# Meta rows side by side, a router fed by unnormed tokens, and the token-row step moved into the experts

## The reference, cut to what matters

```
h = modulate(rms_norm(x, g_ffn[l]), sh_f, sc_f)       # rms * g * (1 + sc) + sh
x = x + gt_f[:, None, :] * moe(h, w_router[l], b_router[l], w1, b1, w2, b2)
return rms_norm(x, g_final)

def moe(h, w_router, b_router, w1, b1, w2, b2):
    logits = xf @ w_router + b_router                 # 256 x 32
    top_val, top_idx = lax.top_k(logits, TOP_K)       # 4 of 32
    gates = jax.nn.softmax(top_val, axis=-1)
    # for each expert e, on its tokens:
    u = xb @ w1[e] + b1[e]
    glu = jnp.minimum(u[:, ::2], 7.0); lin = jnp.clip(u[:, 1::2], -7.0, 7.0)
    a = glu * jax.nn.sigmoid(1.702 * glu) * (lin + 1.0)
    y = a @ w2[e] + b2[e]                             # times its gate, added into x
```

## Time and profile before

| | us |
|---|---|
| median of 3 runs | 1924.18 |
| lowest and highest | 1923.88, 1926.73 |
| the profiled execution: its time | 1924.68 |
| its span, first to last instruction | 1923.0 |
| PE busy | 1826.4 (95%) |
| DVE busy, ACT busy | 800.5 (42%), 593.7 (31%) |
| transfers | 568.65 MB, mean 296 GB/s |

### The profile page before, as it was taken

How to read it: one execution, slowest core, us unless ns; L and a number is a source line. 1 busy time by engine, 2 the same in 40 slices (tenths; PEclk the granted TensorE clock), 3 DMA queues, 4 the chain that set the end, 5 groups by cost and what they waited for, 6 DMA issues and landing times.

```text
span 1923.0 us, 27611 instructions
## 1 busy us (share of the span) xinstructions
PE 1826.4 (95%) x11191; PEld 1224.0 (64%) x11192; DVE 800.5 (42%) x1357; ACT 593.7 (31%) x949; POOL 38.0 (2%) x62
## 2 busy tenths in 40 slices
PE   7999999989998999999899999999999999999996
PEld 6777779989998899899854344344344343343442
DVE  5444556778874544547412122222122122122222
ACT  5665676453435456555410000000000000000001
POOL 2000000000000000000000000000000000000000
PEclk9999999989998999999889999999999999999998
DMA  8333335768783744435759999999999999999995
GB/s 253 98 107 109 111 110 175 241 213 278 273 304 111 250 161 154 153 126 169 292 211 417 428 429 428 429 428 429 428 428 429 428 429 429 428 428 428 429 427 229
DMA packets 147813, 568.65 MB, mean 296 GB/s; under 512 B 6016, under 2 KB 102376, under 8 KB 123040
## 3 DMA queue, kind: packets, MB, share of 16 engines
q1 hardware_dynamic: 139616, 536.60, 70.8%
q0 software_dynamic: 8128, 31.07, 4.7%
HBM read 566.58 MB, written 3.43 MB: 296 GB/s over the span
## 4 chain that ended last, share of the span: by engine, by line
PE 58%; DMA 33%; ACT 4%; DVE 3%; issue 1%; SPq 0%; DVEq 0%; ACTq 0%
DMA s_ring<-in_w_mlp 33%; PE banks L2078 10%; PE banks L1692 9%; PE banks L1694 8%; PE banks L1693 8%; PE banks L1837 3%; PE banks L1838 3%; PE banks L1839 3%; PE banks L2115 3%; PE banks L2088 2%; PE banks L1650 1%; PE banks L2063 1%; ACT r_w2h L718 1%; DVE r_w2l L1110 0%; PE banks L1736 0%
## 5 line engine op out<-in xcount | busy, mean ns | idle before, releaser
L2078 PE MATMUL banks<-s_ring,s_W 128*64 128x512 f32 x2048 | 460.9, 598 | 29.5 <-DMA s_ring<-in_w_mlp 29.5
L2078 PEld LDWEIGHTS banks<-s_ring,s_W 128*64 128x64 f32 x2048 | 139.1, 137 | 331.6 <-issue 258.6
L1046 ACT ACTIVATE s_W<-s_W 128x512 f32<-128x512 f32 x32 | 20.2, 630 | 764.2 <-DVE s_W L1564 764.2
L2115 PE MATMUL banks<-s_ring,s_W 128*64 128x512 f32 x1024 | 226.0, 594 | 0.3 <-ACT s_W L1039 0.3
L1556 DVE TENSOR_TENSOR s_W<-banks,s_W 128x512 f32<-128x512 f32 x32 | 22.1, 692 | 461.0 <-PE banks L2115 461.0
L2115 PEld LDWEIGHTS banks<-s_ring,s_W 128*64 128x64 f32 x1024 | 73.3, 137 | 147.2 <-issue 132.7
L1338 DVE TENSOR_TENSOR r_w2l<-s_ring,r_w2h 128x1024 fp32r<-128x1024 f32 x96 | 116.9, 1223 | 83.3 <-ACT r_w2h L894 83.1
L1110 DVE TENSOR_TENSOR r_w2l<-s_ring,r_w2h 128x1024 fp32r<-128x1024 f32 x88 | 107.5, 1224 | 99.7 <-ACT r_w2h L718 99.2
L1543 DVE TENSOR_TENSOR s_W<-banks,s_W 128x512 f32<-128x512 f32 x128 | 82.2, 684 | 147.7 <-PE banks L2063 147.7
L1692 PE MATMUL banks<-r_x2h,r_w2h 128*128 128x256 f32 x448 | 130.8, 292 | 6.2 <-DVE r_x2l L1354 6.2
L2088 PEld LDWEIGHTS banks<-s_W 128*128 128x128 f32 x1024 | 120.0, 196 | 24.2 <-issue 24.2
(11 more groups left out here) (417 smaller groups left out, 3236.7 us busy)
## 6 DMA issues: line engine op xcount, KB each, us to landing
s_ring<-in_w_mlp SPq DMA_DIRECT2D x192, 2048.0 KB, 22.4
s_ring<-in_w_in SPq DMA_DIRECT2D x62, 1024.0 KB, 5.2
s_ring<-in_w_ada POOLq DMA_DIRECT2D x24, 1024.0 KB, 9.2
s_ring<-in_w_ffn_gate SPq DMA_DIRECT2D x11, 1024.0 KB, 5.4
s_ring<-in_w_ffn_up SPq DMA_DIRECT2D x11, 1024.0 KB, 10.6
s_ring<-in_w_ffn_down SPq DMA_DIRECT2D x5, 2048.0 KB, 10.1
s_ring<-in_w_gate SPq DMA_DIRECT2D x8, 1024.0 KB, 5.3
s_ring<-in_w_br_sb SPq DMA_DIRECT2D x4, 1024.0 KB, 4.8
```

Of the source, the lines that this page charges most:

```text
L2078: last = mm(pb[b][64 * h:64 * h + 64, :], XgT[:, 2 * c + k, :], slot(c, 2)[:, k, 1024 * h + 512 * b:1024 * h + 512 * b + 512], start=False ...
L2115: last = mm(pb[2][64 * h:64 * h + 64, :], aT[:, k, 64 * c:64 * c + 64], slot(4 + c, 4)[:, k, 512 * h:512 * h + 512], start=c == 0 and k == ...
```

## The change

In the first block: the rounded meta rows and their rest are laid side by side (`xm`, 32 columns), so that the meta part of an `sv` or `dv` unit has four products, not six; the meta keys are copied eight times over 128 columns (`skM`, on ACT), as is the triangle (`ntriM`), so that the meta rows of the stick-breaking steps fill 128 partitions and ACT and DVE take 640 columns in one instruction; of the differential steps the meta columns are doubled (`wvM`, on DVE), so that 32 rows sum both halves.

In the second block: the router weights and their bias are scaled by the norm's gain and shift while `o` runs (`router` and `router_bias`, at "wrA" and "wrB"); PE makes the logits from the unnormed residual, one slice behind the squares (`token_square`, `logits`), and the root is taken for each token (two columns). The token rows for the experts are a matmul of `hx` by a diagonal of the gains, scaled by the root when ACT copies them; the shift is added later, on DVE, when `XgT` is copied (`shifted`). Masks and gates are made with broadcast operations over all four choices. The spreads of the output gate come after the counts. The residual rows and the second biases move behind `expert(0)` (`first_sum`), the biases with four row groups of 32. `choose_g(e)` moves into turn e. The final gain is spread by PE at the very end and read by DVE from the banks.

```diff
@@ order2
-                 (unit_of("o") + 2, 1, SQUARED, {"square": 0}))
+                 (unit_of("o") + 2, 1, SQUARED, {"square": 0}),
+                 (unit_of("o"), 1, 1, {"wrA": 1.5, "wrB": 2.5}))
@@ ACT, first block
+        act.activation(xm[:, :, 0:M], xnm, ACT.Copy).then_inc(S["xn_hi"], 1)
...
+                act.activation(skM[:, c, :].rearrange("p (a n) -> p a n", a=KT), copies(src[:, 0:M]), ACT.Copy)
...
-                st.do(act.activation(ex[:, 0:384], ex[:, 0:384], ACT.Exp))
-                st.do(act.activation(ex[0:M, 384:640], ex[0:M, 384:640], ACT.Exp))
+                st.do(act.activation(ex, ex, ACT.Exp))
...
@@ ACT, before the experts
-        root(4, nrms, T)
-        for t in range(KT):
-            act.wait_ge(S["norm_x"], 3 * KT + t + 2)
-            act.activation(hn[:, t, :], hn[:, t, :], ACT.Identity, bias=modT[:, 24 + t:25 + t]).then_inc(S["norm_s"], 1)
-
-        act.wait_ge(S["b1_in"], 64)
+        act.wait_ge(S["norm_ms"], 6)
+        act.activation(root4, pb[3][:, 0:2], ACT.Sqrt, bias=epsc, scale=1.0 / D).then_inc(S["norm_r"], 1)
+        act.wait_ge(S["b1_in"], 128)
         act.activation(b1r[:, :], b1x, ACT.Copy).then_inc(S["b1_split"], 1)
...
         def expert(e, cur, prev):
-            if cur:
-                act.wait_ge(S["gath"], e + 1)
-                since(act, "u_mm", e * 4)
-                act.activation(XgT, pb[3].rearrange("p (a n) -> p a n", a=KT), ACT.Copy).then_inc(S["xg"], 1)
@@ DVE, before the experts
+        choose_b(0)
+        gates()
+        nc.vector.memset(taken, 0.0).then_inc(S["round"], 1)
...
+        tt(b2q, b2q, gty, ALU.mult).then_inc(S["b2_scaled"], 1)
         expert(0, True, False)
@@ DVE, a turn
         def expert(e, cur, prev):
-            if prev:
-                since(dve, "selt_mm", e - 1)
-                choose_g(e - 1)
             if cur:
                 dve.wait_ge(S["gath"], e + 1)
+                since(dve, "u_mm", e * 4)
+                shifted().then_inc(S["xg"], 1)
                 choose_u(e + 1)
+                since(dve, "selt_mm", e)
+                choose_g(e)
@@ PE, first block
             if kind in V_KINDS:
+                for kk in range(2):
+                    for i, w in enumerate((whi, wlo)):
+                        last = mm(pb[groups[0] % 3][0:2 * M, :], xm[:, 2 * (n % 4) + kk, :], w[:, kk, :],
+                                  start=n % 4 == 0 and kk + i == 0, stop=n % 4 == 3 and kk + i == 2)
...
@@ PE, second block
+        def logits(k):
...
+            last = mm(pb[5][0:E, 0:T], wrg[:, k, :], hx[:, k, :], start=k == 0, stop=k == KT - 1)
...
+        def token_square(k):
+            if k >= 1:
+                logits(k - 1)
+            if k == KT - 1:
+                logits(k)
+            pe.wait_ge(S["norm_sq"], KT * 3 + k + 1)
+            for t in range(2):
+                last = mm(pb[3][:, t:t + 1], nsq[:, k, P * t:P * t + P], ones[:, 0:1], start=k == 0 and t == 0, stop=k == KT - 1, skip_group_check=True)
...
+        def first_sum():
+            pe.wait_ge(S["route"], 6)
+            for t in range(2):
+                last = nc.tensor.transpose(pb[2][:, P * t:P * t + P], gat4[:, t, :], ident)
+            last.then_inc(S["gt_mm"], 1)
+            for b in range(4):
+                for j in range(4):
+                    mm(pb[4 + b][:, P * j:P * j + P], hx[:, 4 * (b % 2) + j, P * (b // 2):P * (b // 2) + P], ident,
+                       start=j == 0, stop=False, skip_group_check=True)
+            pe.wait_ge(S["gt_kept"], 1)
+            pe.wait_ge(S["b2_scaled"], 1)
+            for q in range(4):
+                v, t = slice(E * q, E * q + E), q % 2
+                mm(pb[4 + 2 * t + q // 2], gatT[v, P * t:P * t + P], b2q[v, :], start=False, stop=True, skip_group_check=True)\
+                    .then_inc(S["h_mm"], 1)
...
+        pe.wait_ge(S["spread_kept"], 2)
         expert(0, True, False)
-
-        pe.wait_ge(S["acc_init"], 4)
-        for b in range(2):
-            spread(6 + b, vec[:, VROW["g_final"]:VROW["g_final"] + KT], b).then_inc(S["spread"], 1)
+        first_sum()
         expert(1, True, True)
...
         further(pe, again)
+        for b in range(2):
+            spread(4 + b, vec[:, VROW["g_final"]:VROW["g_final"] + KT], b)
```

More of the change, by code:

```diff
@@ L306, in program @@
     mT = area(W, 20864, KT, T)
+    skM, ntriM, wvM = area(W, 20864, HEADS, P), W[0:M, 21888:22016], area(W, 22016, 2, 2 * M)
     zs, ex, sp, la = (lent[:, 640 * n:640 * n + 640] for n in range(4))
@@ L759, in keep1, with copies @@
             act.activation(dst, src, ACT.Copy, scale=scale).then_inc(S["act_evac1"], 1)
+        def copies(ap):
+            return ap.unsqueeze(1).broadcast_to([ap.shape[0], KT, M])
         def sb_step(s, h):
@@ L1048, in _ @@
         expert(0, True, False)
-        for b in range(2):
-            act.wait_ge(S["spread"], b + 3)
-            act.activation(gfb[:, 512 * b:512 * b + 512], pb[6 + b], ACT.Copy).then_inc(S["spread_kept"], 1)
+        first_sum()
         expert(1, True, True)
@@ L1058, in again @@
             act.wait_ge(S["over_pe"], n * 7 + 2)
-            act.activation(XgT, pb[3].rearrange("p (a n) -> p a n", a=KT), ACT.Copy).then_inc(S["over_act"], 1)
+            for k in range(KT):
+                last = act.activation(XgT[:, k, :], pb[3][:, 64 * k:64 * k + 64], ACT.Identity, bias=shift[:, k:k + 1])
+            last.then_inc(S["over_act"], 1)
             act.wait_ge(S["over_pe"], n * 7 + 3)
@@ L1246, in df_step @@
                     v = slice(144 * qt, 144 + 272 * qt)
-                    last = stt(wv[:, v], sc[:, 1, v], sml[:, 25 + 2 * qt:26 + 2 * qt], wv[:, v], ALU.mult, ALU.add)
-                last.then_inc(S["df_w"], 1)
+                    st.do(stt(wv[:, v], sc[:, 1, v], sml[:, 25 + 2 * qt:26 + 2 * qt], wv[:, v], ALU.mult, ALU.add))
+                st.wait()
+                meta = wv[:, 0:288].rearrange("p (a n) -> p a n", a=2)[:, :, 0:M].unsqueeze(2).broadcast_to([P, 2, 2, M])
+                nc.vector.tensor_copy(wvM.rearrange("p a (b n) -> p a b n", b=2), meta).then_inc(S["df_w"], 1)
             if s == "dfD":
@@ L1447, in _ @@
                     keep2(g)
+            elif s == "wrA":
+                router()
+            elif s == "wrB":
+                router_bias()
             elif s == "toep":
@@ L1748, in sb_step @@
                 mm(pb[3][:, T:384], skT[:, h, M + P:TM], q[:, P:T], start=True, stop=True)
-                mm(pb[4][0:M, 0:T], skT[:, h, 0:M], q, start=True, stop=True).then_inc(S["scores"], 1)
+                mm(pb[4][:, 0:T], skM[:, h, :], q, start=True, stop=True).then_inc(S["scores"], 1)
             if s == "sbB":
```

267 lines of the change are left out of this document (149 added, 118 removed).

## The result

The changed kernel takes 1903.67 us (median of four runs, 1899.63 to 1904.73) against 1925.38 for the kernel before beside it: a ratio of 0.988, 95% interval 0.987 to 0.990. It is 21.7 us faster, and 29.9 were forecast; 1903.67 lies just outside the range, which ended at 1903.0. The profiled execution took 1903.53 for a span of 1901.8, 21.2 less than the span before. The kernel before, timed beside each group of experiments, had medians of 1923.8 to 1926.4, so a difference of medians between two groups is uncertain by 1 or 2 us.

A forecast was written before the change was run, and what follows sets the result against it. Expert-weight transfers (428 GB/s) bound the kernel once streaming, PE's pace before the last gemm's end; -10.0 + 4.2 - 27.1 + 2.7 + 0.3 = -29.9, from 1924.2 to 1894.3 us, range 1889.5 to 1903.

The forecast's parts named there:

- First block, -10.0: First block: fewer meta products and 128-row attention steps save 10.0 us, between 5 and 13.
- Between the blocks, nothing: Unchanged norms between the two blocks: the prediction gave them no term, so no change in time.
- While `o` runs, +4.2: Gemm `o` in the second block: added logits, router bias and shift matmuls cost 4.2 us, between 3 and 6.
- E: The end of the last gemm, before the router's tail: 936.4 us before, forecast near 930.6.
- E moves by -5.8: The last gemm's end comes 5.8 us sooner, from -10.0 in the first block and +4.2 while `o` runs.
- If E moves by less than 3 us: A sign that the prediction would be wrong: the last gemm's end moves by under 3 us.
- First w1 product at E + 16.1: Router tail: expert 0's first w1 product starts 16.1 us after the last gemm, 26.0 sooner, set by DVE's queue.
- -27.1 and +2.7: Expert-weight stream: standstill after the last gemm falls from 32 to 4.9 us (-27.1); the gap at expert 1 grows (+2.7).
- End, +0.3: Kernel's end: PE's spread of the final gain, beside the last sums and root, costs 0 to 0.5 us, taken as 0.3.
- the clock rival (1898): Before the first expert PE's clock falls and the gather takes 3.5 us longer: 1898 us, chance 20%.
- The starving stream: At `first_sum`, serial bias matmuls (+2.3 us) and a late ACT copy (+1.5) starve the weight stream: 1898 us, chance 10%.
- the row groups overlapped: In `first_sum`, four bias matmuls on row groups of 32 overlap and take about 1.1 us; serial would cost 2.3 more.

The follow-up runs named there:

- best1: Changed kernel with later square-root table load, final gain spread in last expert turn, first sum inside expert 1, `XgT` ahead of the gates: 1895.05 us.
- serial_bias: Changed kernel with the four second-bias products all reading rows 0 to 31, one row group instead of four (values wrong, same work size): 1907.6 us.
- wide_ada: Changed kernel with the 36 modulation products between the blocks 128 columns wide instead of 1: 1897.4 us.
- best2: Changed kernel with wide modulation products, later table load, `XgT` ahead of the gates, first sum behind expert 0's w2 products, final gain spread in last turn: 1887.33 us.
- each half: The kernel before with only the first block's part of the change, 1918.37 us, or with all the rest alone, 1908.0 us.
- pad32: Changed kernel with 32 more matmuls that nobody reads, in a wait of PE before the second block: 1898.73 us.
- early_spread: Changed kernel with the final gain's spread ahead of the test for a second pass, not behind it: 1895.8 us.

## Why the prediction was wrong, step by step

- *First block, -10.0.* Right: 9.6 at the norms, 9.5 to 9.8 at the first loads of the feed-forward weights and of the second block. Kernels with the same first block differ by up to 2 us here, so the match is no finer than that. The four meta products that remain in a unit take 0.95 us on the chain, 0.24 each. PE's wait for DVE's masked terms fell from 3.3 to 2.7, in seven heads instead of six.
- *Between the blocks, nothing.* Wrong by 3.7. The forecast took unchanged code to cost what it did. This stretch has two lengths, 24.5 and 28.1, by where PE's clock falls; the profile before showed the short one, with the fall in the middle of it. The forecast had no bound for it. Which length the kernel before takes in its other executions is not shown; it has one trace.
- *While `o` runs, +4.2.* Right: from the issue of the first w1 chunks to E it took 25.1 and takes 29.4. Five logits and the bias products cost what rows 6 and 8 gave.
- *E moves by -5.8.* Wrong: 0.3. "If E moves by less than 3 us" was one of the three signs, and it came true though the terms that the sum has up to E were right: 3.7 of the difference are the norms and 1.5 the table load, which both stood at nothing. That load is a line of the diff; the prediction counted that two table loads leave the tail and didn't ask where the preloaded one went, nor who stands behind it on ACT.
- *First w1 product at E + 16.1.* E + 15.3, by the mechanism named: DVE's queue. Putting `XgT` ahead of the gates, in `best1`, made it E + 14.7, with 0.3 us of wait left, so it was worth 0.6.
- *-27.1 and +2.7.* Right by mechanism, and the exact sum, -24.4 in both, is luck: up to the last turn's transposes it was -25.6 (962.1 us from E before, 936.6 after), and the last turn gave 1.2 back, nearly all of it in w2 products at a lower clock (9.14 us against 7.89). Expert 1 starts 9.85 us behind expert 0's last product, 9.6 were forecast, and the next w2 chunks are issued 24.4 us sooner after E. But the 2.7 is not a price of the first sum alone, as the prediction has it: two runs that moved it got back 0 and at most 1.5.
- *End, +0.3.* Wrong by 3.2, the largest miss of a term that the sum names. The forecast hid the spread behind the sums "after its last scatter". It didn't see that PE passes a branch first, and that this branch can take 3.8 us. Before, nothing was behind it on PE, so no row showed it.
- The rivals: the clock rival (1898) named the right resource in the wrong place. In the tail the clock stayed at 1.00 throughout; it fell in the norms, at the end and in the last turn. Its ground, that the clock before was at 0.50 each time after 3 to 4 us of idleness, was read too simply: PE idled from 938.1 to 942.0 and from 958.2 to 961.4, but the clock fell at about 939.4, within the first wait, and at about 963.3, when PE had been at work again for most of 2 us. The starving stream did not come, the row groups overlapped; `serial_bias` shows that it would have been about 4 us had they not, where the prediction priced 2.3.

## What to carry to other kernels

Work moved off a critical tail still has to be looked up at its new place: ask which queue it enters and what stands behind it there, for a table load of 1.3 us as for a spread of 2. Price a stretch whose clock changes in it by both of its lengths, even if its code isn't touched. And if PE must multiply by one column for long, try a wider product: here 128 columns cost 0.005 us a pass more than one, over 72 passes, and the stretch took 21.5 us where it had taken 28.1 or 24.5.

## What the runs showed of the hardware

- PE's granted clock fell while PE was busy all the time with products of one column; with 128 columns it stayed at 1.00 (`wide_ada`, `best2`). It also fell behind eight passes of 32 rows, in one trace.
- The same branch on PE took 0.3 to 0.4 us in two kernels and 3.3 to 3.8 us in six; the two have 32 matmuls more ahead of it.
- Two changes can so cost something together that neither costs alone: from the last scatter to the end each half takes 11.4 us and the whole 14.9, because only together do they put the branch at the slow place.
- A wait of 2.4 us of PE went with the lower clock in five traces and not in four others (the changed kernel, `serial_bias`, `pad32`, `early_spread`). What decides it, and which of the two lengths the norms take, stays open.
